# Two mixers of a hybrid decoder step: attention heads in pairs on the halves of the array, dense products by halves over three banks

## The reference, cut to what matters

```python
# layer 0: sliding-window attention (16 heads, 2 key heads, sinks) beside a Mamba-2 block
scores = einsum('bnqkgd,bnskd->bnqkgs', qb, kb) * dh ** -0.5      # blocks of 128 x 256, head width 64
scores = where(valid, scores + bias, -inf)                        # ALiBi
p, lse = softmax_lse(scores, sink)
o = einsum('bnqkgs,bnskd->bnqkgd', p, vb)
x = x + concatenate([o, y_ssm]) @ even_w_out                      # 3072 -> 1024
x = x + square(relu(rmsnorm(x) @ w_up)) @ w_down                  # 1024 -> 4096 -> 1024
# layer 1: three head groups, (window, dilation) = (128,1), (512,4), (2048,16), 16 heads each
q, k, v = split(rmsnorm(x) @ odd_w_in)                            # 1024 -> 9216
o = sum(softmax(lses) * outs);  x = x + o @ odd_w_out;  x = x + mlp(x)
```

## Time and profile before

| | us |
|---|---|
| median of 3 runs | 2425.16 (2418.47 to 2436.14) |
| profiled execution, span | 2423.7 |
| PE busy | 2251.7 (93%) |
| PE weight loads busy | 2101.5 (87%) |
| DVE busy | 1383.4 (57%) |
| ACT busy | 736.9 (30%) |
| POOL busy | 429.1 (18%) |
| DMA, mean rate | 215 GB/s |

### The profile page before, as it was taken

One profiled execution on the slowest core, in us unless ns is written; L12 is line 12 of the kernel. 1 busy time (PEld: TensorE's weight loads), 2 busy tenths in 40 slices (PEclk: granted clock), 3 DMA queues, 4 the chain that ended last, 5 costly groups with the idle time before them and its releaser, 6 DMA issues.

```text
span 2423.7 us, 41530 instructions
## 1 busy us (share of the span) xinstructions
PE 2251.7 (93%) x17512; PEld 2101.5 (87%) x17512; DVE 1383.4 (57%) x2005; ACT 736.9 (30%) x1408; POOL 429.1 (18%) x287
## 2 busy tenths in 40 slices
PE   7998887788899999999999999999999979999997
PEld 7988776677688999999998987888898858999997
DVE  4786777785644544344565564655646547353444
ACT  3323324345333322122323322332332334221221
POOL 1000322211111100000035334234415400000000
PEclk9998998888999999999999999999999989999998
DMA  4225666772233687777748668568747945877774
GB/s 164 70 83 175 247 234 228 256 237 72 79 126 120 229 276 252 269 261 258 263 156 302 220 218 286 171 217 272 265 158 255 323 171 174 276 263 252 269 260 176
DMA packets 282909, 519.92 MB, mean 215 GB/s; under 512 B 17776, under 2 KB 253664, under 8 KB 278880
## 3 DMA queue, kind: packets, MB, share of 16 engines
q1 hardware_dynamic: 271408, 324.44, 40.9%
q10 hardware_dynamic: 5888, 177.91, 20.1%
q0 software_dynamic: 5440, 15.08, 1.7%
HBM read 483.76 MB, written 210.80 MB: 287 GB/s over the span
## 4 chain that ended last, share of the span: by engine, by line
PE 71%; DVE 12%; DMA 6%; issue 5%; ACT 4%; POOL 1%; SPq 0%; DVEq 0%; ACTq 0%; POOLq 0%
PE gp L2264 33%; PE gp L2799 15%; PE gp L2593 5%; PE gp L2417 4%; DMA uk<-in_dil_k 3%; DVE cacc L1556 2%; DMA decay<-tmp_a_row 2%; PE mp L2684 2%; PE mp L2759 1%; PE mp L2653 1%; POOL uq L2899 1%; PE mp L2515 1%; PE mp L2663 1%; PE mp L2533 1%; PE mp L2502 1%
## 5 line engine op out<-in xcount | busy, mean ns | idle before, releaser
L2264 PE MATMUL gp<-a_hi,w_hi 128*128 128x272 f32 x1456 | 307.1, 292 | 23.3 <-DVE w_lo L1479 12.2
L2264 PE MATMUL gp<-a_hi,w_lo 128*128 128x272 f32 x1456 | 302.5, 289 | 0.0
L2264 PE MATMUL gp<-a_lo,w_hi 128*128 128x272 f32 x1456 | 301.7, 289 | 0.0
L2899 POOL TENSOR_TENSOR uq<-uq,uk 128x1024 f32<-128x1024 f32 x96 | 248.4, 2591 | 299.0 <-DMA uk<-in_dil_k 298.9
L2799 PE MATMUL gp<-a_hi,w_hi 128*128 128x272 f32 x1152 | 257.8, 305 | 0.0
L2264 PEld LDWEIGHTS gp<-a_hi,w_hi 128*128 128x128 f32 x1456 | 230.9, 190 | 26.3 <-DVE cin L1545 13.0
L2799 PE MATMUL gp<-a_lo,w_hi 128*128 128x272 f32 x1152 | 241.5, 291 | 0.0
L2799 PE MATMUL gp<-a_hi,w_lo 128*128 128x272 f32 x1152 | 241.0, 291 | 0.0
L2264 PEld LDWEIGHTS gp<-a_hi,w_lo 128*128 128x128 f32 x1456 | 231.1, 190 | 0.0
L2264 PEld LDWEIGHTS gp<-a_lo,w_hi 128*128 128x128 f32 x1456 | 229.4, 190 | 0.0
L2264 PE MATMUL gp<-b_hi,w_hi 128*128 128x272 f32 x1024 | 212.0, 288 | 0.0
(11 more groups left out here) (384 smaller groups left out, 4093.0 us busy)
## 6 DMA issues: line engine op xcount, KB each, us to landing
out_dil_ks<-in_dil_k ACTq DMA_DIRECT2D x32, 2044.0 KB
out_dil_vs<-in_dil_v ACTq DMA_DIRECT2D x32, 2044.0 KB
uq<-tmp_rows SPq DMA_DIRECT2D x96, 512.0 KB, 6.3
w_raw<-in_odd_w_in SPq DMA_DIRECT2D x36, 1024.0 KB, 8.0
vs<-in_dil_v SPq DMA_DIRECT2D x67, 512.0 KB, 6.7
w_raw<-in_w_up SPq DMA_DIRECT2D x32, 1024.0 KB, 8.1
w_raw<-in_w_down SPq DMA_DIRECT2D x32, 1024.0 KB, 8.1
uk<-in_dil_k SPq DMA_DIRECT2D x64, 512.0 KB, 7.2
```

The lines of the kernel that those rows point to most:

```text
L2264: m = nc.tensor.matmul(gp[:, c, h, 0:HALF], w[:, sl, k, c * P:(c + 1) * P], x[:, k, h * HALF:(h + 1) * HALF], start=n < 2, stop=n >= 46)
L2899: nc.gpsimd.tensor_tensor(uqs[n % 3], uqs[n % 3], k, ALU.mult).then_inc(item_mul, 1)
```

## The change

Four things change, in both mixers.

1. **Scores in pairs.** The steps are renumbered so that p even and p odd are the two heads of a pair, with the same query blocks: p = 4C + 2 pc + head. At the part where p (even) stood, PE runs both heads' matmuls in turns, one on rows 0 to 63 into `mp[:,0]`, the other on rows 64 to 127 into the fourth bank of `gp` (bank 0 in layer 0, bank 3 in layer 1). Nothing of scores is run at the odd step's part. In layer 0 the first two steps stay single.
2. **Values in pairs (layer 0).** `values` runs for both heads at the odd step's part, their matmuls in turns on the two halves of the output rows; `at_pt` becomes two buffers.
3. **Dense products by halves.** Since `gp` gives up a bank, a chunk's half 0 is run over all weight blocks in parts 0 to 3 and half 1 in parts 4 to 7, over three banks in rotation. PE waits at part 4 for `half_drained` (half 0 of the chunk before). Chunk 0 of each mixer, the last third of layer 0's (d = 16 to 23) and the last output projection of layer 1 keep the old order.
4. **Draining by halves.** DVE takes each half out by itself: half 0 in the middle of its slot's queue, half 1 where the whole chunk stood.

```diff
+def mix_bank(d, h):
+    return 1 + (2 * d + h + 1) % 3
+def turning_bank(i, n, h):
+    y = chunk0(i) - chunk0(0) + n
+    return (2 * y + h) % 3
...
-        at_pt = over_a("at_pt", [P, 4, P])
+        at_pt = [over_a("at_pt0", [P, 4, P]), at("at_pt1", S0, [P, 4, P])]
...
+            def add_half(d, h):
+                n, f = d % 8, slice(h * HALF, (h + 1) * HALF)
...
+                dve.wait_ge((mm_half, mm_done)[h], (d + 1, 2 * G0["out0_1"] + d + 1)[h])
+                nc.vector.tensor_tensor(x_t[:, n, f], x_t[:, n, f], gb[:, mix_bank(d, h), 0:HALF],
+                                        ALU.add).then_inc((half_drained, drained)[h], 1)
...
                 for part in range(8):
+                    if part == (6 if s == N_PRE else 4) and 0 <= s - N_PRE < N_TURN:
+                        add_half(s - N_PRE, 0)
...
             def scores(p):
-                C, half, pc = p // 4, p // 2 % 2, p % 2
+                C, pc = p // 4, p // 2 % 2
...
+                heads = [(slice(0, HEAD_DIM), mp[:, 0]), (slice(HEAD_DIM, P), gb[:, 0])]
+                if p < 2:
+                    heads = [(heads[p][0], mp[:, 0])]
                 for t in (2 * pc, 2 * pc + 1):
                     w = 2 * P if t else P
-                    m = nc.tensor.matmul(mp[:, 0, at0:at0 + w], at_q[hp, C % 2, t * P:(t + 1) * P],
-                                         at_k[hp, kv, max(t - 1, 0) * P:(t + 1) * P], start=True, stop=True)
+                    for hp, s in heads:
+                        m = nc.tensor.matmul(s[:, at0:at0 + w], at_q[hp, C % 2, t * P:(t + 1) * P],
+                                             at_k[hp, kv, max(t - 1, 0) * P:(t + 1) * P], start=True, stop=True)
...
             def values(p):
-                pe.wait_ge(t_done, p + 1)
+                pe.wait_ge(t_done, p + 2)
...
+                        for half in range(2):
+                            m = nc.tensor.matmul(mp[half * HEAD_DIM:(half + 1) * HEAD_DIM, 2, t * P:(t + 1) * P], at_v[:, at, f],
+                                                 at_pt[half][:, j], start=(n == 0), stop=(at == t), skip_group_check=True)
...
+                    by_half = 0 < d < N_TURN
+                    if by_half and part == 4:
+                        pe.wait_ge(half_drained, d)
...
+                        if by_half:
+                            steps = [(k, j, part // 4) for k in (part % 4 * 2, part % 4 * 2 + 1) for j in range(3)]
+                        else:
+                            steps = [(part, j, h) for j in range(3) for h in range(2)]
...
-                if part == 7 and z in PIECE:
+                if part == 7 and PIECE.get(z, 1) % 2 == 0:
                     score1(PIECE[z])
...
+                            h, k0 = sub * 2 // subs, sub % (subs // 2) * per_k
+                            steps = [(k, j, h) for k in range(k0, k0 + per_k) for j in range(3)]
+                            if h == 1 and k0 == 0:
+                                pe.wait_ge(half_drained, HALVES_MIX + chunk0(i) - chunk0(0) + n)
...
+                if z < N_SLOTS and ODD[z // 2][0] != "o":
+                    drain(z // 2, z % 2, 0)
                 for n, qd, g, b in ITEM_AT.get(z - 1, ()):
                     item_out(n, qd, g, b)
```

More of the change, by code:

```diff
@@ L177 @@
 N_MIX = N_PRE + 24
+N_TURN = 16
+def mix_bank(d, h):
+    return 1 + (2 * d + h + 1) % 3
 def mix_events():
@@ L561, in build @@
         drained = sem("drained")
+        mm_half = sem("mm_half")
+        half_drained = sem("half_drained")
         consts_in = sem("consts_in")
@@ L2031, in drain, with by4 @@
[L2031 to L2035, removed]
+                    def by4(t):
+                        return t.rearrange("p (n r) -> p n r", r=4)
@@ L2512, in turn @@
                     pe.wait_ge(root_done, 3)
-                for j in range(4 if p % 2 else 3):
-                    tile = j // 2 if p % 2 else (j + 1) // 2
+                four = p % 4 > 1
+                for j in range(4 if four else 3):
+                    tile = j // 2 if four else (j + 1) // 2
                     m = nc.tensor.matmul(mp[:, 1, j * P:(j + 1) * P], at_e[:, p % 2, j], at_f[:, p % 2, tile], start=True, stop=True)
@@ L2661, in turn1 @@
                 wait(pe, o1_done, p)
-                for j in range(3 if p % 16 < 8 and p % 2 == 0 else 4):
+                for j in range(3 if p % 16 < 8 and p % 4 < 2 else 4):
                     m = nc.tensor.transpose(mp[:, 1, j * P:(j + 1) * P], e1[:, j], ident[:])
@@ L2802, in odd_group @@
-                        if k == last_k:
-                            m.then_inc(mm_done, 1)
+                                pe.wait_ge(a_ready, AB[2] + sub + 1)
+                        turning = i < len(ODD) - 1
+                        per_k = (last_k + 1) * 2 // subs
+                        if i == 0 and c == 0 or not turning:
+                            steps = [(k, j, h) for k in range(sub * per_k // 2, (sub + 1) * per_k // 2) for j in range(3) for h in range(2)]
+                        else:
+                            h, k0 = sub * 2 // subs, sub % (subs // 2) * per_k
+                            steps = [(k, j, h) for k in range(k0, k0 + per_k) for j in range(3)]
+                            if h == 1 and k0 == 0:
+                                pe.wait_ge(half_drained, HALVES_MIX + chunk0(i) - chunk0(0) + n)
@@ new lines, in odd_group @@
+                        if sub == 0:
+                            pe.wait_ge(drained, chunk0(i) + n - 1)
+                        for k, j, h in steps:
+                            w, x = ((hi, xs[0]), (lo, xs[0]), (hi, xs[1]))[j]
+                            out = gb[:, turning_bank(i, n, h), 0:HALF] if turning else gp[:, n % 2, h, 0:HALF]
+                            m = nc.tensor.matmul(out, w[:, k, n * P:(n + 1) * P], x[:, k, h * HALF:(h + 1) * HALF],
+                                                 start=k == 0 and j == 0, stop=k == last_k and j == 2)
+                            if k == last_k and j == 2 and (h or turning):
+                                m.then_inc(mm_done if h else mm_half, 1)
```

200 lines of the change are left out of this document (107 added, 93 removed).

## The result

| | before | changed |
|---|---|---|
| median of runs, us | 2430.65 (4 runs) | 2388.27 (4 runs, 2386.47 to 2396.37) |
| ratio, 95% interval | | 0.985 (0.982 to 0.988) |
| span of the profiled execution, us | 2423.7 | 2384.7 |

The account below looks back on a forecast made before the run. Both mixers were taken as bound by PE, but for stalls. Cuts of 33.4 us in layer 0 and 37.7 in layer 1, less 21 of stalls, save 50: 2423.7 becomes 2373.7, median 2375 us; range 2352 to 2404.

Parts of the forecast that it names:

- its return as stalls: Both layers: of 33.4 us cut in layer 0 and 37.7 in layer 1, 21 us come back as stalls.
- Pairs overlap: Scores and values on PE: two heads' matmuls run side by side, so a pair costs what one head did.
- row halves don't overlap: Rival on scores pairs: they save only the 0.4 us of a switch; 29 us saved, 2396; chance 0.12.
- strict order: Rival on PE's paired matmuls: strict FIFO makes eight passes need five steps, not four; 2385; chance 0.10.
- Same bank: Dense products by halves: consecutive matmuls adding into one bank cost nothing, still 125 ns each; the opposing rival had chance 0.04.
- So nothing is queued long behind it: PE's new wait at part 4: for a half finished four parts before, same slack of one chunk's length, so harmless.
- the halves at nothing: Dense products and draining by halves: no cost on PE; DVE's 56 extra pieces, 17 us, fit in its idle time.
- what would prove me wrong: Sign: a large wait for `half_drained` would mean DVE's queue, with new tokens' items between the two halves, is the bound.
- Stalls of layer 1: Layer 1: savings lost to waits, 5.8 us in the first quarter and 7.5 in the later ones.
- The term of the later quarters: Layer 1's later three quarters: full stretches with two or three pairs in each lose their savings, 7.5 us.
- Stalls of layer 0: Layer 0: savings lost to waits, 5 us at the gated norms and 3 us in the steady chunks.
- the stalls take more: Rival: DMA paces layer 1's later quarters, which keeps a third, 12 us; layer 0 keeps 25; 2388 to 2398; chance 0.20.

Follow-up runs that it names:

- e4: Changed kernel, but within each pair of scores all matmuls of the first head are issued before those of the second; 2401.2 us, ratio 0.989.
- e1: Changed kernel without pairs: dense products by halves alone, scores and values of both layers head by head at their old places; 2446.0 us, ratio 1.007 to the kernel before.
- e6: Halves alone, no pairs, as in e1, with DVE taking a chunk's first half behind the new tokens' items in layer 1; 2432.6 us, ratio 1.003.
- e5: Changed kernel, but in layer 1 DVE takes a chunk's first half at its slot's end, behind the new tokens' items; 2383.8 us, ratio 0.983.
- e8: Changed kernel with the edits of e5 (layer 1) and e7 (layer 0) together; 2361.2 us, ratio 0.974.
- e7: Changed kernel, but in layer 0 DVE splits w_lo behind the odd head's scores and makes o_lo behind its sums; 2374.8 us, ratio 0.979.
- e12: e8 with lighter loads in layer 1, cached keys of one token in four, so part of the work is left out; 2345.6 us, ratio 0.967.
- e3: Changed kernel with scores and values of layer 0 head by head at their old places, pairs in layer 1 alone; 2415.6 us, ratio 0.996.

## Why the prediction was right, and where not

The time, 2388, lies in the range and 13 us over the forecast, just outside the 10 us that I gave 0.48. The work cut was sized right (71 us), its return as stalls too small: 32.7 us in the profiles for 21.

- **Pairs overlap: right.** 71 us of PE time are gone, as summed. The rivals "row halves don't overlap" and "strict order" are refuted by the starts in the changed kernel, and e4 started the second head's passes (1392.86) ahead of the first head's that were issued before them (1392.97). The Trainium skill, "TensorE: Matmul & The Clock Gate", section on packing small matmuls, calls matmuls "strict FIFO, no reordering"; this trace differs for matmuls on different row halves, and the measurement decides.
- **Same bank: right.** 126 ns a dense matmul, and 0.01 us more per chunk.
- **"So nothing is queued long behind it", and the halves at nothing: wrong, the step that failed.** I asked who is queued behind PE's new wait, and priced DVE's extra pieces by their length. The wait that costs is the one DVE got: for a half in the middle of a slot, with the items behind it. It makes most of the 17 us by which e1 is slower than the kernel before; moving it takes 10 to 13 of them back (e6). PE's own new wait is small, as forecast: 2.0 us, once, for `q_t` in the changed kernel. I had named this queue only as what would prove me wrong.
- **Stalls of layer 1, 13.3 us: too small by 7.2** (20.5; 17.5 to 22.7 over the three profiles of this layer). The term of the later quarters was slim by its own prices: seven and a half pairs at 37.7 / 32 us are 8.8, not 7.5. With the drain moved (e5) the stage saves 24.2, against 24.4 forecast, but that agreement is luck: the waits fall by 2.2 us only (69.7 to 67.5), the rest is busy time, and so in the spread. That DVE's order is a cause is shown for the halves by e6, and with pairs by e8 against e7 (waits 66.7 to 59.9).
- **Stalls of layer 0, 8 us: too small by 4.2** (12.2). The steady chunk has a wait of 1.1 us per two chunks before a turn, and 0.16 before scores, where I took 3 us in all; I had seen `w_lo` ahead of the scores, not `o_lo` ahead of the sums. A chunk there takes 10.7 us (`w_lo` at 693.79 and at 715.14, two chunks apart), 0.6 of it waits, where I forecast 9.9. e7 shows the cause, in one edit that moves both; which of them pays more wasn't tried.
- The rival "the stalls take more" gave 2388 to 2398, with layer 1 at a third by DMA pace. Its time came true, its mechanism is not borne out: e12 doesn't show the pace of DMA, and layer 0 kept 21 us, not 25. What layer 1 kept does not decide, 17 us in this profile and 9 and 21 in e3 and e7, against its 12 and my 24.4.

## What to carry to other kernels

When work is cut off the bounding engine, list every wait that the change adds on the *other* engines, and for each what is queued behind it in that engine's order; a piece of 0.6 us that costs nothing to run can hold up a chain of loads for 4. Consumers that have slack (a drain with a chunk's time) go behind those that feed a DMA queue. And measure the part of a change that only makes room for the rest by itself: here it cost 17 us that the net gain hid.

## What was not expected of the hardware

- Matmuls on two row halves are not tied to program order. With 4 passes of one head ahead, the other head's start at once (two by two, as when alternating); with 8 ahead, after the fifth, 0.55 us into the pair (1392.31 to 1392.86).
- The granted clock of TensorE went with DVE's order: over the runs it is 0.962 in the kernel before, 0.958 in e1, and 0.961 in e6, which differs from e1 by the place of the drain alone. By the estimate above, the lost clock took more than twice the 7 us of added waits in e1. In its profile the clock stood at 0.50 from 1975 to 1995 us, behind 5 us of which PE had idled 1.7. The amount of idling alone does not tell when it falls: the kernel before idled 2.9 of the 5 us from 1940, and was granted 1.00 in them and in the next 5.
